# A four-layer transformer on one core: the byte distance between weights and activations in three feed-forwards

## The chip, the core and the metric

The kernel runs on one core of one Trainium2 chip. The metric is the device time of one execution in microseconds (us). A core has engines that run their own instruction streams and meet at semaphores: TensorE (PE) multiplies, VectorE (DVE) and ScalarE (ACT) work element by element, GpSimd (POOL) and SyncE (SP) here mostly issue transfers. All of them read the core's on-chip memory of 128 partitions; an address below is a byte address inside a partition.

## The reference

Input `x` is 512 tokens of width 1024, before which 16 learned tokens are put. Four layers follow, each a mixer and then a feed-forward: a recurrent unit with windowed attention, a retention, a gated delta rule, and a dilated attention. All is float32. Every feed-forward has hidden width 2816 and is

```python
def swiglu(h, w_in, w_out):
    gate, up = jnp.split(h @ w_in, 2, axis=-1)
    return (jax.nn.silu(gate) * up) @ w_out

h = (rms_norm(x, norm_ffn[layer]) * (1.0 + sc2) + sh2)
x = x + g2 * swiglu(h, w_ffn_in[layer], w_ffn_out[layer])
```

(the first two layers' feed-forwards have only a gain, and no shift and gate). The 16 learned tokens are dropped at the end; the last three feed-forwards work on the 512 tokens alone, the first one on all 528.

## The kernel before

Activations are kept transposed: the feature index, 128 at a time, is the partition, and the tokens run along the partition, so that a "chunk" of 128 features is 512 tokens, 2048 bytes. The residual stream `x_stream` stays on chip for the whole program.

A float32 product is made of three products of a rounded type (`F32R`): each operand is split in a high part and the rest, and `split_products` (lines 278 to 282) issues high times high (L280), high weights times low rows (L281) and low weights times high rows (L282) into the same accumulator:

```python
    nc.tensor.matmul(out, w_hi, h_hi, start=first, stop=False)
    nc.tensor.matmul(out, w_hi, h_lo, start=False, stop=False)
    return nc.tensor.matmul(out, w_lo, h_hi, start=False, stop=last)
```

In each, the 128 x 128 weights are the stationary operand, loaded by an instruction of its own (LDWEIGHTS, in the profile under PEld), and the rows, 512 tokens, are the moving operand that streams past them. In the profile's names the moving operand stands first: `ps<-up_h_hi,w_hi`.

Weights come from memory in tiles of up to 1 MB into `w_raw`, which has two slots. ACT copies a tile rounded into `w_hi` (`split_hi`, L195), DVE subtracts to get `w_lo` (`split_lo`, L201), and PE uses the tile as soon as `lo_ready` tells it. SP loads the tile after next when a slot is free. All of this is written out by hand: each engine has its own loop over the tiles, and semaphores (`tile_loaded`, `hi_ready`, `lo_ready`, `tile_used`, `psum_free`) join them.

A feed-forward (`feed_forward`, L892) has two parts. The first (`Up`, L777) normalizes the stream into `K.h_hi` and `K.h_lo` (8 chunks each), then goes over 22 tiles of weights; a tile gives one 128-wide chunk of gate and one of up, 2 outputs x 8 chunks x 3 = 48 matmuls. The first tile's 48 products are written by `Normalized.first_products` (lines 462, 463, 469), which has the first chunk in halves, and the other 21 tiles' by `split_products`, 1008 matmuls. ACT and DVE make `silu(gate) * up` and split it into `a_hi` and `a_lo` (22 chunks each). The second part (`add_projected`) multiplies these with the 16 half tiles of the down weights: 8 outputs x 22 chunks x 3 = 528 matmuls, and DVE adds each output to the stream.

Buffers are laid out by nesting: `K.sb` puts each new one right behind the one before it, and leaving a scope gives the space back. `take_h(name, ctx, cols, room)` puts an unused buffer of `room` bytes before `h_hi` and `h_lo`. Its sizes are the only things that shift the buffers of a feed-forward. `w_hi` starts at byte 49,792 and `w_lo` 16,384 bytes behind it, so both lie at 128 modulo 256; the 128 x 128 blocks inside them start 512 or 1024 bytes apart, and the chunks of 512 tokens 2048 bytes apart, all multiples of 256. So in a stage where rows are 512 tokens wide one number describes every matmul: D, the address of the weights minus the address of the moving rows, modulo 256.

| rows (512 wide) | address | D before |
|---|---|---|
| `ret_y`, `gdn_h`, `gdn_y`, `dsw_h` (mixers) | | 192 |
| `dsw_y` (output of the last mixer, 96 matmuls) | 126,272 | 64 |
| rows of feed-forwards 1, 2, 3 (`ffn1_h`, `up_2_h`, `up_3_h`) | 86,208 | 192 |
| activations of feed-forwards 1, 2, 3 (`up_1_act`, `up_2_act`, `up_3_act`) | 118,976 | 192 |

Three stages are different. In feed-forward 0 a chunk is 528 tokens, 2112 bytes, used as two spans of 264 tokens: D goes down by 64 from chunk to chunk and by 32 from the first span to the second, so the first span has D = 192, 128, 64, 0 in turn and the second 160, 96, 32, 224. In the values of the retention (`w_hi,ret_h_hi`) and of the first group of the last mixer (`w_hi,dsw_h_hi`) the roles are exchanged: 256 columns of weights move, and 128 tokens of the rows are stationary. Weights and rows are there 0 and 192 apart.

Of the kernel before, what the change touches and what calls it, by code (L numbers as in the profile page):

```python
# [28 lines left out]
P = 128  # L29
# [29 lines left out]
ONLY_X = (N_META, 1)  # L59
# [6 lines left out]
class Chain:  # L66


    def __init__(self, sem):
        self.sem, self.n = sem, 0  # L70
# [706 lines left out]
class Up:  # L777

    def __init__(self, K, up, cols, norm, side, ctx, cond=False):
        self.K, self.up, self.cols, self.side, self.cond = K, up, cols, side, cond
        W = T - cols[0]
        self.n = {k: v[1] for k, v in K.up.items()}
        self.sems = {k: v[0] for k, v in K.up.items()}
        self.a_hi = K.sb(up.name + "_act_hi", [P, FF_CH, W], F32R, ctx)
        self.a_lo = K.sb(up.name + "_act_lo", [P, FF_CH, W], F32R, ctx)
        self.work = K.sb(up.name + "_work", [P, 3 * W], ctx=ctx)
        self.silu, self.prod = self.work[:, 0:W], self.work[:, W:3 * W].rearrange("p (n w) -> p n w", n=2)
        if side is not None:  # L790
            side.open(ctx)
        gain, shift = norm
        self.norm = Normalized(K, cols, gain, shift, side and side.acc[:].rearrange("p n c -> p (n c)"), ctx)
        for k in K.up:
            K.up[k][1] += up.tiles
# [93 lines left out]
            pe.wait_ge(self.sems["lo"], self.n["lo"] + self.up.tiles)  # L889


def feed_forward(K, up, down, cols, gate=None, side=None, norm=None, stats=True, cond=False, two_ahead=False):  # L892


    with ExitStack() as ctx:
        first = Up(K, up, cols, norm, side, ctx, cond)
        add_projected(K, down, (first.a_hi, first.a_lo), cols, parts=2, base=cols[0], gate=gate, side=side,
                      before=first, stats=Squares(K, cols, first.work, down) if stats else None, two_ahead=two_ahead)


def column_weights(name, matrix, tiles, unroll, cols=256, first=0, split=True):

    rows = matrix.shape[0] // P
    rowwise = matrix.rearrange("(k p) c -> p k c", p=P)

    def source(i, j):
        at = first + j * cols + i * (unroll * cols)
        return [(lambda slot: slot.rearrange("p (k c) -> p k c", k=rows), rowwise[:, :, bass.ds(at, cols)])]
    w = Weights(name, tiles, unroll, (rows, cols), source, split)
    w.loads = 1  # L910
    return w


def up_weights(name, matrix):

    rowwise = matrix.rearrange("(k p) c -> p k c", p=P)

    def source(i, j):
        def part(g):
            return lambda slot: slot.rearrange("p (k g c) -> p k g c", k=DC, g=2)[:, :, g, :]  # L920
        return [(part(g), rowwise[:, :, bass.ds(i * (2 * P) + (j * P + g * D_FF), P)]) for g in range(2)]
    w = Weights(name, FF_CH, 2, (DC, 2 * P), source)
    w.loads = 2
    return w


def down_weights(name, matrix):

    rows = FF_CH // 2
    halves = matrix.rearrange("(h k p) c -> h p k c", p=P, h=2)  # L930

    def source(i, j):
        return [(lambda slot: slot.rearrange("p (k c) -> p k c", k=rows),
                 halves[j % 2][:, :, bass.ds(i * (2 * P) + (j // 2) * P, P)])]
    w = Weights(name, 2 * DC, 4, (rows, P), source)
    w.loads = 1
    return w
# [252 lines left out]
def param(K, name, n):  # L1190
    at = K.at[name]
    return K.cols[:, at:at + n]
# [1951 lines left out]
def delta_rule(K, I, W, mods):  # L3144
    gain, shift, gate = mods
    with ExitStack() as layer:
        rule = DeltaRule(K, I, W, gain, shift, layer)
        stats = Squares(K, ONLY_X, rule.squares, W["gdn_out"])
        add_projected(K, W["gdn_out"], (rule.y_hi, rule.y_lo), ONLY_X, base=N_META, gate=gate, before=rule, stats=stats)
# [637 lines left out]
def two_blocks(nc, I, const, out):  # L3787
    with ExitStack() as ctx:
        K = Core(nc, ctx)
        K.const = const  # L3790
        ab = I["ab_w_in"].rearrange("a d n -> (a d) n")
        ret = I["ret_w_in"].rearrange("a d n -> (a d) n")
        W = {}
        W["ab_x"] = column_weights("ab_x", ab, 2, 2)
        W["ab_q"] = column_weights("ab_q", ab, 2, 2, first=1024)
        W["ab_k"] = column_weights("ab_k", ab, 1, 1, P, first=1536)
        W["ab_v"] = column_weights("ab_v", ab, 1, 1, P, first=1664)
        W["ab_g"] = column_weights("ab_g", ab, 2, 2, first=512)
        W["ab_out"] = column_weights("ab_out", I["ab_w_out"][0], 4, 2)
        W["up_0"], W["down_0"] = up_weights("up_0", I["ffn_w_gu"][0]), down_weights("down_0", I["ffn_w_down"][0])  # L3800
        W["ret_k"] = column_weights("ret_k", ret, 4, 2, first=D)
        W["ret_q"] = column_weights("ret_q", ret, 4, 2)
        W["ret_v"] = column_weights("ret_v", ret, 8, 2, first=2 * D)
        W["ret_g"] = column_weights("ret_g", ret, 8, 2, first=4 * D)
        W["ret_out"] = column_weights("ret_out", I["ret_w_out"][0], 8, 2, P)
        W["up_1"], W["down_1"] = up_weights("up_1", I["ffn_w_gu"][1]), down_weights("down_1", I["ffn_w_down"][1])
        gdn = I["gdn_w_in_2"].rearrange("a d n -> (a d) n")
        W["gdn_k0"] = column_weights("gdn_k0", gdn, 1, 1, first=D)
        W["gdn_ab"] = gate_weights("gdn_ab", gdn)
        W["gdn_k"] = column_weights("gdn_k", gdn, 3, 3, first=D + 256)  # L3810
        W["gdn_q"] = column_weights("gdn_q", gdn, 4, 2)
        W["gdn_v"] = column_weights("gdn_v", gdn, 4, 2, first=2 * D)
        W["gdn_z"] = column_weights("gdn_z", gdn, 4, 2, first=3 * D)
        W["gdn_out"] = column_weights("gdn_out", I["gdn_w_out_2"][0], 4, 2)
        W["up_2"], W["down_2"] = up_weights("up_2", I["w_ffn_in_2"][0]), down_weights("down_2", I["w_ffn_out_2"][0])
        dsw = I["dsw_w_in_2"].rearrange("a d n -> (a d) n")
        W["dsw_qk"] = column_weights("dsw_qk", dsw, 12, 2)
        for g in range(3):
            W["dsw_v%d" % g] = column_weights("dsw_v%d" % g, dsw, 2, 2, first=3072 + g * 512)
        W["dsw_out"] = column_weights("dsw_out", I["dsw_w_out_2"][0], 2, 2, 512)  # L3820
        W["up_3"], W["down_3"] = up_weights("up_3", I["w_ffn_in_2"][1]), down_weights("down_3", I["w_ffn_out_2"][1])
        K.plan(list(W.values()))

        prologue(K, I, list(W.values())[0])
        with ExitStack() as layer:
            K.take_h("ab_h", layer)
            gate = K.sb("ab_gate", [P, LRU_CH, T], ctx=layer)
            norm = Normalized(K, ALL, param(K, "norm_ab", 8), space=gate[:].rearrange("p c w -> p (c w)"))
            mixer = Mixer(K, I, W, norm, gate, layer)
            add_projected(K, W["ab_out"], (K.h_hi, K.h_lo), ALL, before=mixer, stats=Squares(K, ALL, mixer.work, W["ab_out"]))  # L3830
        K.end_layer()
        with ExitStack() as layer:
            K.take_h("ffn0_h", layer)
            feed_forward(K, W["up_0"], W["down_0"], ALL, norm=(param(K, "norm_ffn", 16)[:, 0:8], None), cond=True)
        retention(K, W)
        K.end_layer()
        mods = [Modulation(K, I, 0, ctx)]
        with ExitStack() as layer:
            K.take_h("ffn1_h", layer, ONLY_X, 960)
            feed_forward(K, W["up_1"], W["down_1"], ONLY_X, side=mods[0],  # L3840
                         norm=(param(K, "norm_ffn", 16)[:, 8:16], None), two_ahead=True)
        delta_rule(K, I, W, mods[0].parts(0))
        K.end_layer()
        mods.append(Modulation(K, I, 1, ctx))
        modulated_feed_forward(K, W["up_2"], W["down_2"], mods[0].parts(1), mods[1])
        dilated_attention(K, I, W, mods[1].parts(0))
        K.end_layer()
        modulated_feed_forward(K, W["up_3"], W["down_3"], mods[1].parts(1), stats=False)
        store(K, out)


def modulated_feed_forward(K, up, down, mods, side=None, stats=True):
    gain, shift, gate = mods
    with ExitStack() as layer:
        K.take_h(up.name + "_h", layer, ONLY_X, 896)
        feed_forward(K, up, down, ONLY_X, gate, side, (gain, shift), stats)


def store(K, out):
# [50 lines left out]
```

## Time and profile before

| | |
|---|---|
| median of three runs | 3008.45 us (3006.57 to 3008.66) |
| profiled execution, first to last instruction | 3006.2 us |
| PE busy | 2891.8 us (96%) |
| PE weight load busy | 2484.8 us (83%) |
| DVE busy | 1437.2 us (48%) |
| ACT busy | 1121.2 us (37%) |
| POOL busy | 118.6 us (4%) |
| mean granted clock of PE | 0.985 |

The span is one execution. "Busy" of an engine is the time in which at least one of its instructions was under way. A matmul's duration in this profile is from its start to a modelled end, and matmuls overlap: what PE gets done is read from the distance between the starts of two matmuls, not from a duration. Stages are given in us from the start of the span: feed-forward 1 has its 1008 products from 1132.2 to 1370.0 and its 528 from 1370.1 to 1496.7; feed-forward 2 from 1916.3 to 2154.0 and 2154.2 to 2280.3; feed-forward 3 from 2644.1 to 2874.7 and 2875.0 to 2995.6.

### The profile page before, as it was taken

To read this page: it belongs to the slowest core of one execution; us is meant where nothing else is said; L and a number is where in the kernel's file an instruction comes from. 1 tells how busy PE (TensorE), PEld (TensorE's weight loads), DVE (VectorE), ACT (ScalarE), POOL (GpSimd) and SP (SyncE) were. 2 spreads that over 40 slices of the span, in tenths; PEclk is the share of its full clock that TensorE was granted. 3 is DMA by queue.
4 is the path that set the end of the run, shared out by engine and by line. 5 is a ranking of instruction groups with operands and counts; after the bars stand their busy time and mean duration, and the time that the engine had idled before them with its cause. 6 is when DMAs were issued, how large, how long until landed. Compare 5 with 4: busy or idle time off the path is not lost. (4 is left out here: it accounts for less than half of the span.)

```text
span 3006.2 us, 39600 instructions
## 1 busy us (share of the span) xinstructions
PE 2891.8 (96%) x16454; PEld 2484.8 (83%) x16454; DVE 1437.2 (48%) x1613; ACT 1121.2 (37%) x1551; POOL 118.6 (4%) x116
## 2 busy tenths in 40 slices
PE   8989999999999899999999988999999999899999
PEld 8889999998987587888877787788887887778887
DVE  5664333233513734444477745545455865643322
ACT  5444332132232324331265434343224446543321
POOL 0000000001300000000000010000001310000000
PEclk9999999999999999999999999999999999999999
DMA  4212332322222135556432220455563431033322
GB/s 132 66 43 71 92 90 77 97 95 92 70 84 71 28 95 147 156 154 175 132 105 85 70 43 29 112 161 155 166 181 101 112 99 32 18 95 98 94 87 86
DMA packets 409379, 292.70 MB, mean 97 GB/s; under 512 B 24851, under 2 KB 388180, under 8 KB 409250
## 3 DMA queue, kind: packets, MB, share of 16 engines
q1 hardware_dynamic: 403210, 286.68, 32.8%
q0 software_dynamic: 1600, 3.55, 0.8%
q8 instruction: 95, 1.56, 0.2%
q10 hardware_dynamic: 4440, 0.64, 0.2%
q14 instruction: 34, 0.28, 0.0%
HBM read 286.16 MB, written 4.13 MB: 97 GB/s over the span
## 5 line engine op out<-in xcount | busy, mean ns | idle before, releaser
L201 DVE TENSOR_TENSOR w_lo<-w_raw,w_hi 128x2048 fp32r<-128x2048 f32 (+2 forms) x237 | 498.9, 2105 | 523.5 <-ACT w_hi L195 523.0
L195 ACT ACTIVATE w_hi<-w_raw 128x2048 fp32r<-128x2048 f32 (+2 forms) x237 | 416.4, 1757 | 261.8 <-PE ps L282 152.0
L280 PE MATMUL ps<-ffn_h_hi,w_hi 128*128 128x264 f32 (+1 forms) x1008 | 324.9, 322 | 5.2 <-DVE w_lo L201 5.2
L282 PE MATMUL ps<-ffn_h_hi,w_lo 128*128 128x264 f32 (+1 forms) x1008 | 324.0, 321 | 0.0
L281 PE MATMUL ps<-ffn_h_lo,w_hi 128*128 128x264 f32 (+1 forms) x1008 | 322.8, 320 | 0.0
L282 PE MATMUL ps<-up_act_hi,w_lo 128*128 128x512 f32 (+1 forms) x880 | 307.5, 349 | 0.0
L280 PE MATMUL ps<-up_act_hi,w_hi 128*128 128x512 f32 (+1 forms) x880 | 307.1, 349 | 0.2 <-DVE w_lo L201 0.2
L281 PE MATMUL ps<-up_act_lo,w_hi 128*128 128x512 f32 (+1 forms) x880 | 306.4, 348 | 0.0
L280 PE MATMUL ps<-up_h_hi,w_hi 128*128 128x512 f32 x672 | 263.1, 392 | 4.8 <-DVE w_lo L201 4.8
L282 PE MATMUL ps<-up_h_hi,w_lo 128*128 128x512 f32 x672 | 265.1, 394 | 0.0
L281 PE MATMUL ps<-up_h_lo,w_hi 128*128 128x512 f32 x672 | 263.3, 392 | 0.0
L833 DVE TENSOR_TENSOR up_work<-up_work,ps 128x512 f32<-128x512 f32 (+1 forms) x88 | 60.9, 692 | 422.4 <-ACT up_work L814 422.4
L814 ACT ACTIVATE up_work<-ps 128x512 f32<-128x512 f32 (+1 forms) x88 | 53.0, 602 | 527.2 <-PE ps L282 527.1
L280 PEld LDWEIGHTS ps<-ffn_h_hi,w_hi 128*128 128x128 f32 x1008 | 190.5, 189 | 19.0 <-DVE w_lo L201 5.8
L281 PEld LDWEIGHTS ps<-ffn_h_lo,w_hi 128*128 128x128 f32 x1008 | 190.9, 189 | 14.3
L282 PEld LDWEIGHTS ps<-ffn_h_hi,w_lo 128*128 128x128 f32 x1008 | 190.8, 189 | 14.1
L281 PEld LDWEIGHTS ps<-up_act_lo,w_hi 128*128 128x128 f32 x880 | 165.4, 188 | 22.3
L280 PEld LDWEIGHTS ps<-up_act_hi,w_hi 128*128 128x128 f32 x880 | 165.4, 188 | 21.7 <-DVE w_lo L201 0.6
L282 PEld LDWEIGHTS ps<-up_act_hi,w_lo 128*128 128x128 f32 x880 | 165.6, 188 | 21.2
L280 PEld LDWEIGHTS ps<-up_h_hi,w_hi 128*128 128x128 f32 x672 | 126.6, 188 | 32.9 <-DVE w_lo L201 5.7
L281 PEld LDWEIGHTS ps<-up_h_lo,w_hi 128*128 128x128 f32 x672 | 126.5, 188 | 29.0
L282 PEld LDWEIGHTS ps<-up_h_hi,w_lo 128*128 128x128 f32 x672 | 126.6, 188 | 26.6
(580 smaller groups left out, 5620.4 us busy)
## 6 DMA issues: line engine op xcount, KB each, us to landing
mod_raw<-in_w_ada_dram SPq DMA_DIRECT2D x128, 384.0 KB, 4.0
w_raw<-in_ffn_w_gu_dram SPq DMA_DIRECT2D x88, 512.0 KB, 5.2
w_raw<-in_w_ffn_in_dram SPq DMA_DIRECT2D x88, 512.0 KB, 5.2
w_raw<-in_ret_w_in_dram SPq DMA_DIRECT2D x24, 1024.0 KB, 5.2
w_raw<-in_ffn_w_down_dram SPq DMA_DIRECT2D x32, 704.0 KB, 4.9
w_raw<-in_w_ffn_out_dram SPq DMA_DIRECT2D x32, 704.0 KB, 4.9
w_raw<-in_dsw_w_in_dram SPq DMA_DIRECT2D x18, 1024.0 KB, 5.1
w_raw<-in_gdn_w_in_dram SPq DMA_DIRECT2D x16, 1024.0 KB, 5.7
```

What stands on the lines that cost most here:

```text
L195: self.nc.scalar.activation(self.w_hi[:, s, 0:w.size], self.raw[:, s, 0:w.size], ACT.Copy).then_inc(self.hi_ready, 1)
L201: self.nc.vector.tensor_tensor(self.w_lo[:, s, 0:w.size], self.raw[:, s, 0:w.size], self.w_hi[:, s, 0:w.size].bitcast(F32), ALU.subtract). ...
L280: nc.tensor.matmul(out, w_hi, h_hi, start=first, stop=False)
L281: nc.tensor.matmul(out, w_hi, h_lo, start=False, stop=False)
L282: return nc.tensor.matmul(out, w_lo, h_hi, start=False, stop=last)
L814: nc.scalar.activation(K.spans(self.silu, self.cols), K.out_psum((j % 2) * 2, self.cols), ACT.Silu).then_inc(sems["silu"], 1)
L833: nc.vector.tensor_tensor(K.spans(self.prod[:, j % 2, :], self.cols), K.spans(self.silu, self.cols), K.out_psum((j % 2) * 2 + 1, self.cols ...
```

## The change

No instruction is added, removed or reordered; only buffers move. `room` before the rows gets new sizes (960 to 896 bytes; 896 to 768; 896 to 800), and a second unused buffer, `act_room`, of 128, 160 and 64 bytes comes between the rows and the activations.

| matmuls | buffer | address before | after | D before | D after |
|---|---|---|---|---|---|
| 1056 | `ffn1_h_hi`, `_lo` | 86,208 | 86,144 | 192 | 0 |
| 528 | `up_1_act_hi`, `_lo` | 118,976 | 119,040 | 192 | 128 |
| 1056 | `up_2_h_hi`, `_lo` | 86,208 | 86,080 | 192 | 64 |
| 528 | `up_2_act_hi`, `_lo` | 118,976 | 119,008 | 192 | 160 |
| 1056 | `up_3_h_hi`, `_lo` | 86,208 | 86,112 | 192 | 32 |
| 528 | `up_3_act_hi`, `_lo` | 118,976 | 118,944 | 192 | 224 |

(Addresses are those of `_hi`; `_lo` starts a multiple of 256 bytes behind.) What stands behind the activations in the same scope moves with them by 64, 32 or 32 bytes: `up_n_work`, the buffers of the modulation (`mod_raw`, `mod_acc`) in feed-forwards 1 and 2, and `normed_8` in feed-forward 3.

```diff
-    def __init__(self, K, up, cols, norm, side, ctx, cond=False):
+    def __init__(self, K, up, cols, norm, side, ctx, cond=False, act_room=0):
...
+        if act_room:
+            K.sb(up.name + "_act_room", [P, act_room // 4], ctx=ctx)
         self.a_hi = K.sb(up.name + "_act_hi", [P, FF_CH, W], F32R, ctx)
...
-            K.take_h("ffn1_h", layer, ONLY_X, 960)
+            K.take_h("ffn1_h", layer, ONLY_X, 896)
             feed_forward(K, W["up_1"], W["down_1"], ONLY_X, side=mods[0],
-                         norm=(param(K, "norm_ffn", 16)[:, 8:16], None), two_ahead=True)
+                         norm=(param(K, "norm_ffn", 16)[:, 8:16], None), two_ahead=True, act_room=128)
...
-        modulated_feed_forward(K, W["up_2"], W["down_2"], mods[0].parts(1), mods[1])
+        modulated_feed_forward(K, W["up_2"], W["down_2"], mods[0].parts(1), mods[1], h_room=768, act_room=160)
...
-        modulated_feed_forward(K, W["up_3"], W["down_3"], mods[1].parts(1), stats=False)
+        modulated_feed_forward(K, W["up_3"], W["down_3"], mods[1].parts(1), stats=False, h_room=800, act_room=64)
...
-def modulated_feed_forward(K, up, down, mods, side=None, stats=True):
+def modulated_feed_forward(K, up, down, mods, side=None, stats=True, h_room=0, act_room=0):
     gain, shift, gate = mods
     with ExitStack() as layer:
-        K.take_h(up.name + "_h", layer, ONLY_X, 896)
-        feed_forward(K, up, down, ONLY_X, gate, side, (gain, shift), stats)
+        K.take_h(up.name + "_h", layer, ONLY_X, h_room)
+        feed_forward(K, up, down, ONLY_X, gate, side, (gain, shift), stats, act_room=act_room)
```

## Rows read from the trace of the kernel before

**Rows 1.** The page: span, and busy time of the engines.

```profile
span 3006.2 us, 39600 instructions
PE 2891.8 (96%) x16454; PEld 2484.8 (83%) x16454; DVE 1437.2 (48%) x1613; ACT 1121.2 (37%) x1551; POOL 118.6 (4%) x116
```

**Rows 2.** Groups by form, PE: line, names, shapes, count | busy, mean ns | idle before.

```profile
L280 PE MATMUL ps<-up_h_hi,w_hi 128*128 128x512 f32 x672 | 263.1, 392 | 4.8 <-DVE w_lo L201 4.8
...
L280 PE MATMUL ps<-up_act_hi,w_hi 128*128 128x512 f32 x528 | 207.0, 392 | 0.2 <-DVE w_lo L201 0.2
...
L280 PE MATMUL ps<-ffn_h_hi,w_hi 128*128 128x512 f32 x336 | 132.8, 395 | 2.8 <-DVE w_lo L201 2.8
```

**Rows 3.** Windows, PE: stretch, length, busy (count), clock, DMA share, GB/s.

```profile
1132.20:1370.00 237.80, 237.73 (x1056) 0.99 0.55 156
1370.10:1496.70 126.60, 126.40 (x576) 1.00 0.56 160
1916.30:2154.00 237.70, 237.63 (x1055) 0.99 0.55 156
2154.20:2280.30 126.10, 126.10 (x577) 1.00 0.57 166
2644.10:2874.70 230.60, 230.53 (x1007) 1.00 0.35 96
2875.00:2995.60 120.60, 120.60 (x528) 1.00 0.27 78
```

**Rows 4.** Timeline, PE and PEld, feed-forward 2, D 192: start, duration, instruction.

```profile
2099.81 0.39 PE L282 MATMUL ps<-up_h_hi,w_lo 128*128 128x512 f32 x1
2099.81 0.19 PEld L280 LDWEIGHTS ps<-up_h_hi,w_hi 128*128 128x128 f32 x1
...
2102.79 0.39 PE L280 MATMUL ps<-up_h_hi,w_hi 128*128 128x512 f32 x1
...
2108.28 0.39 PE L280 MATMUL ps<-up_h_hi,w_hi 128*128 128x512 f32 x1
```

**Rows 5.** Timeline, PE, output product of the last mixer, D 64, 24 matmuls apart.

```profile
2603.87 0.40 PE L280 MATMUL ps<-dsw_y_hi,w_hi 128*128 128x512 f32 x1
...
2609.47 0.40 PE L280 MATMUL ps<-dsw_y_hi,w_hi 128*128 128x512 f32 x1
```

**Rows 6.** Timeline, PE, values, roles exchanged: distance 0, then 192; 15 matmuls apart.

```profile
797.95 0.28 PE L280 MATMUL ps<-w_hi,ret_h_hi 128*128 128x256 f32 x1
...
799.75 0.28 PE L280 MATMUL ps<-w_hi,ret_h_hi 128*128 128x256 f32 x1
...
2439.95 0.28 PE L280 MATMUL ps<-w_hi,dsw_h_hi 128*128 128x256 f32 x1
...
2441.65 0.28 PE L280 MATMUL ps<-w_hi,dsw_h_hi 128*128 128x256 f32 x1
```

**Rows 7.** Timeline, PE, feed-forward 0: starts of five outputs in turn, 24 matmuls apart.

```profile
375.99 0.28 PE L280 MATMUL ps<-ffn_h_hi,w_hi 128*128 128x264 f32 x1
...
378.88 0.29 PE L280 MATMUL ps<-ffn_h_hi,w_hi 128*128 128x264 f32 x1
...
381.81 0.28 PE L280 MATMUL ps<-ffn_h_hi,w_hi 128*128 128x264 f32 x1
...
384.70 0.29 PE L280 MATMUL ps<-ffn_h_hi,w_hi 128*128 128x264 f32 x1
...
387.64 0.28 PE L280 MATMUL ps<-ffn_h_hi,w_hi 128*128 128x264 f32 x1
```

**Rows 8.** The page, groups: the splits of the weight tiles on DVE and ACT.

```profile
L201 DVE TENSOR_TENSOR w_lo<-w_raw,w_hi 128x2048 fp32r<-128x2048 f32 (+2 forms) x237 | 498.9, 2105 | 523.5 <-ACT w_hi L195 523.0
L195 ACT ACTIVATE w_hi<-w_raw 128x2048 fp32r<-128x2048 f32 (+2 forms) x237 | 416.4, 1757 | 261.8 <-PE ps L282 152.0
```

**Rows 9.** Timeline, PE, third mixer's projections, D 192, 20 matmuls apart.

```profile
1577.04 0.40 PE L281 MATMUL ps<-gdn_h_lo,w_hi 128*128 128x512 f32 x1
...
1581.71 0.40 PE L280 MATMUL ps<-gdn_h_hi,w_hi 128*128 128x512 f32 x1
```

More of the change, by code:

```diff
@@ L889, in row_ready, with feed_forward @@
             pe.wait_ge(self.sems["lo"], self.n["lo"] + self.up.tiles)
-def feed_forward(K, up, down, cols, gate=None, side=None, norm=None, stats=True, cond=False, two_ahead=False):
+def feed_forward(K, up, down, cols, gate=None, side=None, norm=None, stats=True, cond=False, two_ahead=False,
+                 act_room=0):
     with ExitStack() as ctx:
-        first = Up(K, up, cols, norm, side, ctx, cond)
+        first = Up(K, up, cols, norm, side, ctx, cond, act_room)
         add_projected(K, down, (first.a_hi, first.a_lo), cols, parts=2, base=cols[0], gate=gate, side=side,
```

## The prediction

> **What bounds the kernel now.** I read the page's busy times first, then the groups by form, then windows over the stages that the change touches, then the timeline inside them. PE is busy for 2891.8 of 3006.2 us, DVE for 48%, ACT for 37% [rows 1]. The reader is to see that these stages have hardly any idle time to give back or to hide in: over the whole program PE stood idle for 4.8, 2.8 and 0.2 us in total before the first products of the rows and activations [rows 2]. The six stages of the change take 237.8, 126.6, 237.7, 126.1, 230.6 and 120.6 us, together 1079.4 us, at a granted clock of 0.99 to 1.00, that is at the 2.4 GHz level throughout [rows 3]. So the time of a stage is the number of its matmuls times the distance between two starts. In the cleanest stage, the rows of feed-forward 3, 1007 matmuls lie in 230.60 us, 229.0 ns apiece, and in a steady piece 24 matmuls take 2108.28 - 2102.79 = 5.49 us, 228.8 ns [rows 3, 4]. At 2.4 GHz, 512 columns by themselves are 213.3 ns. Some 15.5 ns per matmul are something else. The load of the next weights starts within 10 ns of the matmul that it runs beside, and reads the same memory at the same time [rows 4]. Whether these two reads disturb each other, and how that depends on D, is the whole question, because the change does nothing else.
>
> **The change, part by part.** It adds and removes no instruction on any engine or queue. It changes D for 1056 + 528 matmuls in each of three feed-forwards, 4752 in all (1008 by the shared helper and 48 of the first tile, then 528). I price each new D against D = 192 with the nearest rows.
>
> *D = 64, rows of feed-forward 2, 1056 matmuls.* The trace has this very case: the last mixer's output product, 512 columns, D = 64. There 24 matmuls take 2609.47 - 2603.87 = 5.60 us, 233.3 ns [rows 5]. Against 228.9 (the middle of the two figures above) that is 4.4 ns more: 1056 x 4.4 = 4.6 us.
>
> *D = 0, rows of feed-forward 1, 1056 matmuls.* The nearest row has the roles exchanged, 256 columns of weights moving over 128 stationary tokens. At distance 0, 15 matmuls take 799.75 - 797.95 = 1.80 us, 120.0 ns; at distance 192 they take 2441.65 - 2439.95 = 1.70 us, 113.3 ns [rows 6]. That is 6.7 ns for distance 0, an upper end; the lower end is nothing, as the roles differ. I take half, 3.3 ns: 3.5 us.
>
> *D = 128, activations of feed-forward 1, 528 matmuls.* No row has it alone. Between nothing and the 4.4 ns of D = 64 I take 2.2 ns: 1.2 us.
>
> *D = 32, 160, 224: rows of feed-forward 3, activations of 2 and 3, 2112 matmuls.* These are odd multiples of 32. Feed-forward 0 has them side by side with the even ones: its four outputs per tile are the same 24 matmuls of 264 columns, the first and third over D = 192, 128, 64, 0, the second and fourth over 160, 96, 32, 224. They take 2.89, 2.93, 2.89 and 2.94 us [rows 7]. This is 2.0 ns per matmul for an odd multiple over the mean of the even ones. The mean of the even ones is itself above D = 192, by (0 + 4.4 + 3.3 + 2.2) / 4 = 2.5 ns on my prices. So the term lies between 2.0 and 4.5 ns, or higher if 512 columns pay more often than 264. I take 3.3 ns: 2112 x 3.3 = 7.0 us.
>
> *Everything else costs nothing.* The splits of the weight tiles read and write buffers that don't move; one tile of 48 matmuls is 48 x 229 = 11.0 us of PE, against 2105 ns of DVE and 1757 ns of ACT for the split [rows 8]. The elementwise work on moved buffers has the rest of 11 us as cover. If that cover were gone, PE would wait on `w_lo` at L201, which it does for 4.8 us in total now [rows 2]. The modulation's transfer buffers move by 64 and 32 bytes; DMA is busy for 0.55 of feed-forwards 1 and 2 [rows 3], and a tile is asked for two tiles ahead, so a small slowdown there is hidden as well. A slower PE makes this cover larger. Nothing waits on PE that could turn its delay into more than itself: it adds one to one.
>
> Sum: 4.6 + 3.5 + 1.2 + 7.0 = 16.3 us. The profiled execution has a span of 3006.2 us, 2.3 us under the median of 3008.45; the terms are differences, so I add them to the median: 3024.8 us.
>
> A rule of the Trainium skill speaks against all of this. The page "TensorE: Matmul & The Clock Gate", section "Step-by-step: what each phase is for", says that the engine has two independent read ports into on-chip memory and that loading the next weights "doesn't steal SBUF read bandwidth from the running matmul". By it D would be without effect, and the sum would be 0. The trace disagrees in part: equal matmuls differ with their addresses in rows 7 (2.89 against 2.93 and 2.94 us) and rows 6.
>
> **The rivals.**
>
> *A: D does not decide, the time stays.* The mechanism is that a stream of matmuls falls into one of several steady rhythms after each interruption, and the rhythm, not the address, sets the distance. For it: at D = 192, in the third mixer, 20 matmuls take 1581.71 - 1577.04 = 4.67 us, 233.5 ns, the same as at D = 64 [rows 9]. So the one row from which I priced D = 64 may be a rhythm too. Against it: at D = 192 this rhythm is rare, since the cleanest stage of 1007 matmuls averages 229.0 ns [rows 3], while feed-forward 0 repeats its 2.89 and 2.93 us output after output [rows 7]. It gives 3008.5 us, within 0.2% (6 us) of now; 0.2% is also about what a measurement of this kernel can tell from no change. The independent ports of the skill's page lead to the same time. Chance 0.17, with the cases in which gains and losses of the six stages cancel.
>
> *B: faster.* Some distances may be better than 192. The smallest excess over pure streaming in my rows is 113.3 - 106.7 = 6.6 ns (256 columns at 2.4 GHz are 106.7 ns) [rows 6], against 15.6 ns at 512 columns and D = 192. If the four distances without a row of their own at any width (32, 128, 160, 224; 2640 matmuls) reached it, they would give 2640 x 9.0 = 23.8 us back, while D = 64 and D = 0 still cost 8.1 us: 2992.8 us. It decides once the mean over the 4752 matmuls is below 229 ns, and counts as faster from 1.3 ns below. Against it: rows 7 puts the odd distances above the even ones. Chance 0.07.
>
> *C: a larger loss.* With 512 columns the moving read meets the load at more points than with 264, and every distance but 64 may pay the full 6.7 ns of rows 6: 3696 x 6.7 + 4.6 = 29.4 us, 3037.9 us; at 9 ns for the odd ones it would be 3042.7 us. For it: at 264 columns the four even distances are mixed and each lasts three matmuls only, so that rows 7 may hide much of a steady effect. Against it: no 512-column row of the trace has more than 233.5 ns. Chance 0.12.
>
> *D: the change does not do what it says.* The address arithmetic gives the six distances exactly, and no rule moves the buffers back. I give this nothing.
>
> **How the numbers follow.** The forecast (a loss between 6 and 27 us, likeliest 16.3) has 0.64, C 0.12, A 0.17, B 0.07. Slower by over 0.2% is 0.64 + 0.12 = 0.76, within it 0.17, faster 0.07. The range must leave out 2 in 10 at most. Its low end is 3009: D = 64 as in rows 5 and nothing else would be 3013.1, and I reach into A down to its centre. Its high end is 3037, just under C as worked out. That leaves out B, the lower half of A and most of C's upper part.
>
> **What would show it.** In the windows of rows 3, taken again after the change, the stages should grow by 1056 x 3.3 = 3.5 us (rows of feed-forward 1), 1.2 (its activations), 4.6 and 1.7 (feed-forward 2), 3.5 and 1.7 (feed-forward 3). The timeline should show 233.3 ns per matmul in the rows of feed-forward 2, steadily, and between 229 and 236 elsewhere; the stages of the mixers and of feed-forward 0, which keep their addresses, should not move. PE's idle time before L280 should stay under 5 us per group, and the clock at 0.99 to 1.00. I am wrong in the mechanism if the rows of feed-forward 2 keep 229 ns, wrong in the sizes if one of the stages gains or if one pays over 6.7 ns per matmul, and wrong about the cover if DVE or ACT becomes what PE waits for.

## The result, and the profile after

The changed kernel takes 3019.44 us (median of 4 runs, 3015.91 to 3021.02), against 3007.84 us for the kernel before in the same comparison (median of 4, 3006.57 to 3008.66). The ratio is 1.004, with a 95% interval of 1.0027 to 1.0052: 11.6 us slower, where 16.3 us were forecast. The two lines of the page that answer to [rows 1], of the changed kernel:

```profile
span 3018.6 us, 39600 instructions
PE 2903.2 (96%) x16454; PEld 2483.4 (82%) x16454; DVE 1437.1 (48%) x1613; ACT 1120.6 (37%) x1551; POOL 118.7 (4%) x116
```

Same instructions on every engine, 11.4 us more of busy PE, nothing on DVE and ACT. The six stages of the change, as windows of the changed kernel (stretch, length, PE busy with count, clock, DMA share, GB/s), which answer to [rows 3]:

```profile
1132.90:1368.40 235.50, 235.50 (x1055) 0.99 0.55 158
1368.70:1496.50 127.80, 127.80 (x576) 1.00 0.55 158
1913.50:2155.50 242.00, 241.99 (x1056) 0.99 0.54 153
2155.70:2284.00 128.30, 128.30 (x577) 1.00 0.56 163
2648.20:2884.80 236.60, 236.60 (x1008) 0.99 0.34 94
2885.00:3008.00 123.00, 123.00 (x529) 1.00 0.26 77
```

Line by line against [rows 3] that is -2.3, +1.2, +4.3, +2.2, +6.0 and +2.4 us, together +13.8 us. The first line is the surprise: the rows of feed-forward 1, now at D = 0, got faster. Of the fifth line's 6.0 us only some 4.5 come from D. The clock of that window is 0.99 where it was 1.00 before. PE has just waited 3.0 us for `w_lo`, and soon after that seven matmuls start 427 ns apart, at the 1.2 GHz level:

```profile
2648.77 0.63 PE L282 MATMUL ps<-up_h_hi,w_lo 128*128 128x512 f32 x1
2649.20 0.63 PE L280 MATMUL ps<-up_h_hi,w_hi 128*128 128x512 f32 x1
```

Before, such a stretch fell into the first tile, ahead of the window, where it only made the wait that follows shorter; inside the window it costs about 1.6 us.

The span grew by 12.4 us, so some 1.4 us came back elsewhere. The largest piece is the core of the third mixer, between its projections and its output product, where this change moves nothing. That stretch took 118.2 us before, at a granted clock of 0.93, and 115.4 us after, at 0.95. In the kernels below that do not edit this mixer it took 113.4 us (clock 0.96, lo_apart) to 119.2 us (0.92, halves). So its length goes mostly with the time that PE spends at the 1.2 GHz level in it, though not exactly (both_shifted has 115.9 us at 0.93). A smaller piece goes the other way: the first of the two weight tiles in the values of the last mixer, which keeps its addresses, went from 113.6 to 117.8 ns per matmul, 0.4 us more.

The timeline of the changed kernel shows the two new rhythms (start, duration, instruction). First the rows of feed-forward 1, D = 0, 21 matmuls apart; then the rows of feed-forward 3, D = 32, 24 matmuls apart:

```profile
1304.03 0.39 PE L280 MATMUL ps<-ffn_h_hi,w_hi 128*128 128x512 f32 x1
...
1308.79 0.39 PE L280 MATMUL ps<-ffn_h_hi,w_hi 128*128 128x512 f32 x1
...
2749.68 0.40 PE L282 MATMUL ps<-up_h_hi,w_lo 128*128 128x512 f32 x1
...
2755.28 0.40 PE L282 MATMUL ps<-up_h_hi,w_lo 128*128 128x512 f32 x1
```

4.76 us / 21 = 226.7 ns, and 5.60 us / 24 = 233.3 ns. Taking the mean distance of two starts over a whole stage, gaps of 260 ns and more left out, the changed kernel has 226.9 (D = 0), 232.5 (128), 233.3 (64), 233.3 (160), 233.3 (32) and 233.3 ns (224), where the kernel before had 228.9 to 229.0 in all six. The excess over 512 columns at 2.4 GHz (213.3 ns) was 15.6 ns and is 13.6 ns at D = 0, 19.2 ns at 128 and 20.0 ns at the other four.

### The profile page after: what moved, and what is told of

The parts are those of the page before. It is cut to its first block and busy times, and to the rows that moved or that the text cites. A ratio compares the mean times of both kernels' runs of the same rounds, so it can differ in the third digit from the quotient of the medians.

```text
span 3018.6 us, 39600 instructions
## 1 busy us (share of the span) xinstructions
PE 2903.2 (96%) x16454; PEld 2483.4 (82%) x16454; DVE 1437.1 (48%) x1613; ACT 1120.6 (37%) x1551; POOL 118.7 (4%) x116
## 5 line engine op out<-in xcount | busy, mean ns | idle before, releaser
L280 PE MATMUL ps<-ffn_h_hi,w_hi 128*128 128x264 f32 (+1 forms) x1008 | 323.9, 321 | 5.2 <-DVE w_lo L201 5.2
L282 PE MATMUL ps<-ffn_h_hi,w_lo 128*128 128x264 f32 (+1 forms) x1008 | 322.9, 320 | 0.0
L280 PE MATMUL ps<-up_act_hi,w_hi 128*128 128x512 f32 (+1 forms) x880 | 309.9, 352 | 0.0
L282 PE MATMUL ps<-up_act_hi,w_lo 128*128 128x512 f32 (+1 forms) x880 | 308.2, 350 | 0.0
L280 PE MATMUL ps<-up_h_hi,w_hi 128*128 128x512 f32 x672 | 267.6, 398 | 6.1 <-DVE w_lo L201 6.1
L282 PE MATMUL ps<-up_h_hi,w_lo 128*128 128x512 f32 x672 | 267.1, 398 | 0.0
L280 PEld LDWEIGHTS ps<-ffn_h_hi,w_hi 128*128 128x128 f32 x1008 | 190.5, 189 | 19.0 <-DVE w_lo L201 5.9
L282 PEld LDWEIGHTS ps<-ffn_h_hi,w_lo 128*128 128x128 f32 x1008 | 190.8, 189 | 13.3
L282 PEld LDWEIGHTS ps<-up_act_hi,w_lo 128*128 128x128 f32 x880 | 165.6, 188 | 24.4
L280 PEld LDWEIGHTS ps<-up_act_hi,w_hi 128*128 128x128 f32 x880 | 165.4, 188 | 23.4 <-DVE w_lo L201 0.2
L280 PEld LDWEIGHTS ps<-up_h_hi,w_hi 128*128 128x128 f32 x672 | 127.1, 189 | 37.4 <-DVE w_lo L201 7.0
L282 PEld LDWEIGHTS ps<-up_h_hi,w_lo 128*128 128x128 f32 x672 | 126.9, 189 | 30.8
```

## The experiments

Where a kernel starts from the kernel before or from the changed one, the diff is against that. Means "per matmul" are distances between starts as above, worked out from every start in the trace of the one profiled execution of a kernel. Lines left out of a code cut are marked "...". "Before" in each comparison is 3006 to 3008 us.

### All feed-forwards at distance 0

```diff
-                         norm=(param(K, "norm_ffn", 16)[:, 8:16], None), two_ahead=True, act_room=128)
+                         norm=(param(K, "norm_ffn", 16)[:, 8:16], None), two_ahead=True, act_room=0)
...
-        modulated_feed_forward(K, W["up_2"], W["down_2"], mods[0].parts(1), mods[1], h_room=768, act_room=160)
+        modulated_feed_forward(K, W["up_2"], W["down_2"], mods[0].parts(1), mods[1], h_room=832, act_room=0)
...
-        modulated_feed_forward(K, W["up_3"], W["down_3"], mods[1].parts(1), stats=False, h_room=800, act_room=64)
+        modulated_feed_forward(K, W["up_3"], W["down_3"], mods[1].parts(1), stats=False, h_room=832, act_room=0)
```

> Rows and activations of all three feed-forwards at D = 0. Theory T1 (D alone sets the distance between two matmul starts; D = 0 gives 226.8 ns, as the rows of feed-forward 1 showed after the change): all six stages at 226.8 ns, 4752 x (229.0 - 226.8) = 10.5 us less than the kernel before, about 2997.4 us, and some 22 us less than the changed kernel. Rival T2 (the rhythm is a matter of the stage, of what stands around it, not of D): only the rows of feed-forward 1 at 226.8 ns, the activations still at 232 to 233 ns and the rows of 2 and 3 at 229 to 233 ns, 3007 to 3019 us.

2998.71 us (median of 6) against 3007.59, ratio 0.9967 (0.9955 to 0.9979): 8.9 us faster than before, and faster than the changed kernel. Windows of this run, the same six stages:

```profile
1132.20:1367.80 235.60, 235.58 (x1056) 0.99 0.55 158
1368.00:1493.70 125.70, 125.37 (x577) 1.00 0.56 161
1912.90:2148.50 235.60, 235.55 (x1055) 0.99 0.56 158
2148.80:2274.40 125.60, 125.28 (x576) 1.00 0.56 167
2639.10:2867.50 228.40, 228.39 (x1007) 1.00 0.35 97
2867.80:2987.20 119.40, 119.40 (x528) 1.00 0.27 79
```

Each is shorter than before, by 2.2, 0.9, 2.1, 0.5, 2.2 and 1.2 us: 9.1 us together. All six have 226.7 to 227.1 ns per matmul. T1 holds, T2 falls; the total is 8.9 us less where T1 had 10.5. The first two feed-forwards' activations gain less than the 1.2 us of the third, as they share PE with the sums of the modulation, and waits take part of it.

### The distances dealt out anew

```diff
-            K.take_h("ffn1_h", layer, ONLY_X, 896)
+            K.take_h("ffn1_h", layer, ONLY_X, 768)
...
-                         norm=(param(K, "norm_ffn", 16)[:, 8:16], None), two_ahead=True, act_room=128)
+                         norm=(param(K, "norm_ffn", 16)[:, 8:16], None), two_ahead=True, act_room=32)
...
-        modulated_feed_forward(K, W["up_2"], W["down_2"], mods[0].parts(1), mods[1], h_room=768, act_room=160)
+        modulated_feed_forward(K, W["up_2"], W["down_2"], mods[0].parts(1), mods[1], h_room=832, act_room=64)
...
-        modulated_feed_forward(K, W["up_3"], W["down_3"], mods[1].parts(1), stats=False, h_room=800, act_room=64)
+        modulated_feed_forward(K, W["up_3"], W["down_3"], mods[1].parts(1), stats=False, h_room=736, act_room=32)
```

> The distances dealt out anew: feed-forward 1 rows 128, activations 96; feed-forward 2 rows 0, activations 192; feed-forward 3 rows 96, activations 64. T1: 232.5 ns for the rows of feed-forward 1, 226.8 for the rows of 2, 229.0 for the activations of 2, 233.3 for the activations of 3; D = 96 was in no 512-wide stage so far, by its neighbours 64 and 128 some 233 ns. T2: each stage keeps what it had after the change, 226.8, 232.5, 233.3, 233.3, 233.3, 233.3.

One run, 3021.4 us. Windows:

```profile
1132.40:1371.90 239.50, 239.47 (x1055) 1.00 0.55 155
1372.10:1500.90 128.80, 128.80 (x576) 1.00 0.55 157
1920.40:2155.80 235.40, 235.40 (x1056) 0.99 0.56 158
2156.00:2282.60 126.60, 126.36 (x576) 1.00 0.56 165
2649.80:2885.80 236.00, 236.00 (x1007) 1.00 0.34 94
2886.10:3009.00 122.90, 122.90 (x528) 1.00 0.27 77
```

Per matmul: 232.4 (128), 234.2 (96), 226.7 (0), 229.0 (192), 234.3 (96), 233.3 ns (64). Every distance took its rhythm along to its new stage; feed-forward 2's rows went from 242.0 to 235.4 us and its activations from 128.3 to 126.6. D = 96 is the worst multiple of 32. In these six stages D decides, and the stage does not.

### Weights and rows moved together

```diff
+        self.sb("w_shift", [P, 16])
         self.raw = self.sb("w_raw", [P, 2, SLOT])
```

> The kernel before with 64 unused bytes ahead of the weight buffers, so that weights and rows both move by 64 bytes and every D stays. T1: every stage as before, 229.0 ns in the three feed-forwards and 233.3 ns in the last mixer's output product; about 3008 us. Rival T3 (the absolute address of the rows decides, not the distance): the rows move as they did from D 192 to 128, so the feed-forwards go to 232.5 ns, 4752 x 3.5 = 16.6 us more.

One run, 3007.0 us. Windows of the last output product (D = 64) and of feed-forward 3 (D = 192):

```profile
2595.90:2618.50 22.60, 22.55 (x99) 1.00 0.17 46
2642.90:2873.50 230.60, 230.60 (x1007) 1.00 0.35 96
2873.70:2994.40 120.70, 120.70 (x529) 1.00 0.27 78
```

The two stages of feed-forward 3 are as in [rows 3] to 0.1 us, at 228.9 ns, with every address 64 bytes further, and feed-forward 2 and the activations of feed-forward 1 have 228.9 to 229.0 ns as well. T3 falls, since it had 232.5 ns for all of them: the distance counts, and this shift of the absolute addresses changed nothing.

One stage is not as before, which T1 alone does not explain. The rows of feed-forward 1 (D = 192, as ever) took 0.9 us more than in [rows 3] (first the window, then starts from its timeline; line 281 is L280 of the kernel before):

```profile
1133.20:1371.90 238.70, 238.70 (x1056) 0.99 0.56 156
...
1150.21 0.40 PE L281 MATMUL ps<-ffn_h_hi,w_hi 128*128 128x512 f32 x1
...
1155.81 0.40 PE L281 MATMUL ps<-ffn_h_hi,w_hi 128*128 128x512 f32 x1
...
1200.39 0.39 PE L281 MATMUL ps<-ffn_h_hi,w_hi 128*128 128x512 f32 x1
...
1205.88 0.39 PE L281 MATMUL ps<-ffn_h_hi,w_hi 128*128 128x512 f32 x1
```

The pairs are 24 matmuls apart: 5.60 us, 233.3 ns each, in the first five weight tiles (240 matmuls), and 5.49 us, 228.8 ns each, in the rest. The change comes at 1190.8 us, where twelve small matmuls of the modulation interrupt the stream. So one stage with one D can run in either of two rhythms; the one at D = 192 that [rows 9] shows for some 50 matmuls can last much longer.

### Fewer stationary columns

```diff
...
-                        hi[:, k, m * P:(m + 1) * P], lo[:, k, m * P:(m + 1) * P],
+                        hi[:, k, m * P:m * P + held], lo[:, k, m * P:m * P + held],
```

with `held` 64 in the up products and 32 in the down products, and the output on as many partitions; otherwise the changed kernel.

> The changed kernel with fewer stationary columns in its last three feed-forwards: 64 of 128 in the up products and 32 of 128 in the down products (the other output features are not computed, so the output is not the reference's). The load of the weights is then a half and a quarter as long; the moving operand stays 512 columns. T1a (the excess over 213.3 ns is made of collisions of the moving read with the load of the next weights, 6.7 ns each, two or three of them in a load of 128 columns): about half the excess with 64 columns, 218 to 224 ns, and 213 to 220 ns with 32. Rival T4 (the excess belongs to the matmul and its addresses, whatever the load's length): the intervals of the changed kernel, 226.8, 232.5, 233.3, 233.3, 233.3, 233.3.

One run, 3015.1 us. Windows of the rows of feed-forward 1 and the activations of feed-forward 3, and one of the loads in the latter:

```profile
1132.50:1369.40 236.90, 236.90 (x1056) 1.00 0.55 157
2879.80:3002.80 123.00, 123.00 (x529) 1.00 0.27 77
...
L280 PEld LDWEIGHTS ps<-up_act_hi,w_hi 128*32 128x32 f32 x174 | 18.8, 108 | 21.8
```

A load's record falls from 188 ns (128 columns) to 134 (64) and 108 ns (32), and not to a half and a quarter as the expectation had it.

Per matmul: 230.0 (D = 0, 64 columns), 230.7 (128, 32), 232.0 (64, 64), 233.2 (160, 32), 231.7 (32, 64), 233.3 ns (224, 32). T1a fails: with half or a quarter of the weights to load the excess is not half or a quarter but 16.7 to 20.0 ns, and at D = 0 it even rose from 13.6 to 16.7 ns. T4 comes nearer (two stages are the same to 0.1 ns), though four moved by 1.3 to 3.1 ns, so the load seems to have some part in the rhythm. A caution comes from a stage that this run leaves alone, the output product of the third mixer (D = 192). Its matmuls, once at 2.4 GHz, are 233.3 ns apart to the end of the stage (24 matmuls in 5.60 us), where the other kernels with D = 192 there have 228.9 to 229.0 ns:

```profile
1859.65 0.40 PE L280 MATMUL ps<-gdn_y_hi,w_hi 128*128 128x512 f32 x1
...
1865.25 0.40 PE L280 MATMUL ps<-gdn_y_hi,w_hi 128*128 128x512 f32 x1
```

A shift of a few ns in a single stage of a single run can thus be a change of rhythm and nothing else.

### Half as many moving columns

```diff
...
+                        for a in (0, 256):
+                            mm = split_products(
+                                nc, K.ps[:, (j % 2) * 2 + m, a:a + 256],
+                                hi[:, k, m * P:(m + 1) * P], lo[:, k, m * P:(m + 1) * P],
+                                K.h_hi[:, k, a:a + 256], K.h_lo[:, k, a:a + 256], k == 0 and a == 0, k == DC - 1 and a == 256)
```

and the same in the down products, from all_zero.

> As all_zero, but the 512 moving columns of the products in the last three feed-forwards (after their first weight tile) go in two matmuls of 256 columns, at D = 0. It does the same arithmetic with twice the matmuls. If the excess is one sum per matmul (226.7 - 213.3 = 13.4 ns): 106.7 + 13.4 = 120.1 ns per matmul, so 240 ns for what took 226.7, and 4608 x 13.4 = 62 us more. If it goes with the columns: 113.3 ns per matmul, and the total stays at 2999 us.

One run, 3059.4 us, 60.7 us over all_zero where 62 were expected. Windows of feed-forward 3:

```profile
2677.00:2920.40 243.40, 243.37 (x2015) 0.99 0.33 91
2920.50:3047.10 126.60, 126.60 (x1057) 1.00 0.26 75
```

The down products start 120 ns apart, every one of them, and so do the up products once the clock is at 2.4 GHz (their window begins with a stretch at 1.2 GHz). That is 106.7 + 13.3 ns: the excess is paid once per matmul, and is the same for 256 and 512 columns at D = 0.

### Low weights 64 bytes apart from high ones

```diff
+        self.sb("w_lo_shift", [P, 16])
         self.w_lo = self.sb("w_lo", [P, 2, SLOT], F32R)
```

from all_zero, with 64 bytes less room before the rows.

> As all_zero, but the low halves of the weights 64 bytes behind the high ones modulo 256, so that in the feed-forwards the high weights are at 0 and the low weights at 64 from the rows. Theory T5 (the moving read of one matmul meets the load of the next one's weights): of the three products, L280 and L282 run beside a load of high weights and keep 226.7 ns to the next start, L281 runs beside the load of low weights and gets about 233.3 ns. Rival T6 (a matmul's own weights and rows decide): L282, the one with low weights, is the long one. In both cases the mean is near 228.9 ns, and the total near 3008 us, unless a disturbed product throws its neighbours out of rhythm as well; that would show as a mean above 230 ns.

One run, 3025.6 us, where both theories had some 3008. Its total also holds the mixers, whose rows moved with everything behind the weights and went from 228.9 to 233.2 ns. In the timeline of the down products of feed-forward 3 (lines 281 to 283 are L280 to L282 of the kernel before):

```profile
2949.96 0.39 PE L282 MATMUL ps<-up_act_lo,w_hi 128*128 128x512 f32 x1
2950.19 0.40 PE L283 MATMUL ps<-up_act_hi,w_lo 128*128 128x512 f32 x1
2950.43 0.39 PE L281 MATMUL ps<-up_act_hi,w_hi 128*128 128x512 f32 x1
```

The product with low weights is followed after 0.24 us, the others after 0.23. Over the stage: 228.3, 229.1 and 235.9 ns, mean 231.1. The long one is the product whose own weights are at 64, as T6 said and T5 did not; but the two at D = 0 lost 1.6 and 2.4 ns against the 226.7 ns of all_zero as well, and the mean is 231.1 ns where both theories had 228.9. The expectation had named a mean above 230 ns as the sign that a disturbed product throws its neighbours out of rhythm too.

### The same, and the low rows apart too

```diff
+        if room > 256 and name != "dsw_h":
+            self.sb(name + "_lo_shift", [P, 16], ctx=ctx)
         self.h_lo = self.sb(name + "_lo", [P, DC, pitch or T - cols[0]], F32R, ctx)
...
+        if act_room:
+            K.sb(up.name + "_act_lo_shift", [P, 16], ctx=ctx)
         self.a_lo = K.sb(up.name + "_act_lo", [P, FF_CH, W], F32R, ctx)
```

The rooms before rows and activations are changed so that the high rows keep D = 0.

> As lo_apart (low weights 64 bytes behind the high ones), and the low rows and low activations of the last three feed-forwards moved by the same 64 bytes. Now L281 (high weights, low rows; line 281 or 282 of this kernel) has its own weights and rows at D = 192, L282 (low weights, high rows) at 64, L280 at 0. But each matmul's moving rows and the weights loaded beside it, which are the next matmul's, are again all at distance 0: high rows with high weights, low rows with low weights, high rows with high weights. T5 (the moving read meets the load of the next weights): 226.8 ns for all three, as in all_zero. T6 (a matmul's own weights and rows decide): the product with low weights stays long, near 235 ns, and the one with low rows goes to 229 or more; a mean of 230 ns or above, as in lo_apart (230.9 to 231.2) or worse.

One run, 3028.7 us. The same place in its timeline (lines 283 to 285):

```profile
2949.93 0.39 PE L285 MATMUL ps<-up_act_hi,w_lo 128*128 128x512 f32 x1
2950.16 0.40 PE L283 MATMUL ps<-up_act_hi,w_hi 128*128 128x512 f32 x1
2950.39 0.39 PE L284 MATMUL ps<-up_act_lo,w_hi 128*128 128x512 f32 x1
```

Over the stage 232.6 (own distance 0), 231.7 (192) and 229.1 ns (64), mean 231.1. T5 falls for good: pairing each moving read with the next load at distance 0 does not bring 226.8 back. T6 said 230 ns or above for the mean, which came, but has the order wrong: now the product with low weights is the short one. Its mean is not a sum of single prices either: own distances of 0, 192 and 64 would give (226.8 + 229.0 + 233.3) / 3 = 229.7 ns. So neither simple pairing explains the single intervals. What the runs do give is a mean for a stage in which all three distances are equal.

### Distances that are no multiple of 32

```diff
+        whole = self.sb(name, [P, chunks * cols + 64], F32R, ctx)
+        return whole[:, nudge // 4:nudge // 4 + chunks * cols].rearrange("p (c w) -> p c w", c=chunks)
```

> Distances that are no multiple of 32, by starting the rows inside a longer buffer: feed-forward 1 rows 16, activations 240; feed-forward 2 rows 48, activations 208; feed-forward 3 rows 4, activations 8. Theory T7 (what counts is whether the rows start on the same 64-byte piece grid as the weights: 0, 64, 128, 192 are special): 4, 8, 16, 48, 208 and 240 all cost as much as 32 or 224, 233.3 ns. Rival T8 (the cost changes smoothly with the distance, so that near 0 it is near that of 0): 4 and 8 stay at 227 ns, 16 and 240 lie between 227 and 233, 48 between those of 32 and 64.

One run, 3024.6 us. Windows of the rows of feed-forward 1 and of the two stages of feed-forward 3:

```profile
1133.60:1376.60 243.00, 242.98 (x1056) 1.00 0.54 153
2656.00:2889.90 233.90, 233.86 (x1008) 0.99 0.34 95
2890.10:3012.10 122.00, 122.00 (x529) 1.00 0.27 77
```

Per matmul: 235.8 (16), 231.6 (240), 234.6 (48), 232.1 (208), 230.6 (4), 231.5 ns (8). T7 falls: 4 and 8 cost less than 32. T8 is right about the order near 0 for 4, 8 and 240 but not about the size: one float off costs 3.8 ns already, and 16 is worse than 32, as 48 is worse than 32 and 64. The 235.8 ns of D = 16 are a mean of two rhythms, as in both_shifted: the first 240 matmuls are 233.3 ns apart, and those behind the first sums of the modulation 236.7 ns.

All distances seen with 512 moving rows, with the mean of a stage. Those for 4, 8, 16, 32, 48, 160, 208, 224 and 240 come from one stage in one kernel each (leaving out narrow), and after both_shifted and narrow a difference of a few ns between two of these is not sure to be one of D. 0, 64, 96, 128 and 192 came in two stages or more:

| D | 0 | 4 | 8 | 16 | 32 | 48 | 64 | 96 | 128 | 160 | 192 | 208 | 224 | 240 |
|---|---|---|---|---|---|---|---|---|---|---|---|---|---|---|
| ns | 226.8 | 230.6 | 231.5 | 235.8 | 233.3 | 234.6 | 233.3 | 234.3 | 232.5 | 233.3 | 229.0 | 232.1 | 233.3 | 231.6 |

### The mixers at distance 0 as well

```diff
-            K.take_h("ret_h", inputs, ALL, 192, 576)
+            K.take_h("ret_h", inputs, ALL, 128, 576)
...
-        K.sb("gdn_line_rest", [P, 8], ctx=ctx)
+        K.sb("gdn_line_rest", [P, 56], ctx=ctx)
...
+        K.sb("dsw_y_room", [P, 16], ctx=layer)
         y = [K.sb("dsw_y_" + n, [P, ATT_CH, SEQ], F32R, layer) for n in ("hi", "lo")]
```

The feed-forwards are as in all_zero.

> All feed-forwards at D = 0 as in the run all_zero (2998.7 us), and in addition the third mixer's rows and gated values and the last mixer's output rows at D = 0 (from 192, 192, 64) and the retention's rows at D = 0 in its 512-wide stages (from 192), which puts its values, with exchanged roles, at 64 instead of 0. If the distance is all that counts: 984 x 2.2 = 2.2 us from the third mixer, 576 x 2.2 = 1.3 us from the retention, 96 x 6.6 = 0.6 us from the last output product, and from the values of the retention (120.0 ns now, 768 matmuls of 128 stationary columns) between nothing and 5.1 us, as the only other distance seen there, 192, has 113.3 ns. 2989.5 to 2994.6 us. If another distance inside the mixers (their small matmuls, whose addresses move with them) costs as much as this gives, 2998.7 us or more.

2988.0 us (median of 6) against 3006.96, ratio 0.9933 (0.9917 to 0.9949): it beats both kernels, and all_zero, and lies 1.5 us under the range that was expected. Windows of the retention's values, its gate and the third mixer's projections:

```profile
734.50:845.00 110.50, 110.50 (x960) 1.00 0.25 81
847.50:934.50 87.00, 86.99 (x384) 1.00 0.31 97
1502.30:1716.80 214.50, 209.55 (x941) 1.00 0.28 79
```

and the same stages of the kernel before:

```profile
735.00:851.30 116.30, 116.28 (x960) 0.99 0.24 77
853.90:941.70 87.80, 87.79 (x384) 1.00 0.31 96
1514.50:1729.80 215.30, 211.00 (x940) 1.00 0.28 79
```

The largest piece is the values, where the roles are exchanged: 116.3 to 110.5 us, of which 1.6 is the clock (0.99 against 1.00; permuted, with the same addresses there and clock 1.00, has 114.7 us) and 4.2 the move of that distance from 0 to 64, most intervals falling from 120 to 113 ns. The gate and the projections give 0.8 us each, and the last output product 0.3 (22.5 to 22.2 us). Of the 10 us between the two ratios these windows and the retention's queries (0.4 us) account for 6.5. Much of the rest of the profiled execution is the core of the third mixer: 113.9 us here, at a clock of 0.96, against 118.0 in all_zero. Its moved addresses aren't needed for that: lo_apart, which does not edit this mixer, has 113.4 us at the same clock, and the next run, with the addresses of this one, has 115.1 us at 0.94.

### The last mixer's rows too

```diff
-                K.take_h("dsw_h", proj, ONLY_X, 896)
+                K.take_h("dsw_h", proj, ONLY_X, 832)
```

on top of the kernel of the run before.

> As the run mixers (2988.0 us), with the last mixer's rows at D = 0 instead of 192 as well. Its 720 matmuls of 512 columns should go from 229.1 to 226.8 ns, 1.7 us less; its 192 with exchanged roles go from distance 192 (113.5 ns) to 0, at which the retention's values had 120.0 ns, 1.2 us more. Together 0.4 us less, which no comparison of total times here can tell from nothing; the stages' own lengths should show both.

2990.86 us (median of 5) against 3006.15, ratio 0.9944 (0.9930 to 0.9957), not to be told from the run before it. Windows of the last mixer's 512-wide projections and of its values:

```profile
2281.80:2411.70 129.90, 129.90 (x572) 1.00 0.44 115
2411.90:2435.70 23.80, 23.80 (x196) 1.00 0.17 55
```

In the run before they were 131.2 and 22.6 us: 1.3 us gained by the products with moving rows and 1.2 us lost by those with exchanged roles, both as expected. So the best distance depends on the product: 0 is best for 512 moving rows, and the worst of the three seen (0, 64, 192) for 256 moving columns of weights.

## Why the prediction was right, and where it was not

**What bounds the kernel** held. PE's time per matmul is all there is to change, it adds one to one, and the clock stayed at 0.99 to 1.00 in the six stages. Of what keeps its addresses, the core of the third mixer moved by 2.8 us all the same, with its clock. The cover held too: DVE and ACT are as busy as before, and PE's waits on `w_lo` before L280 over the whole program (engine and line, what it waited for, us in total, times, longest) are, for the kernel before and for the changed one:

```profile
PE ps L280 <- DVE w_lo L201: 11.6, 7, 3.2
```

```profile
PE ps L280 <- DVE w_lo L201: 13.0, 7, 3.0
```

That is 1.4 us more, small beside the 13.8 us of the windows, and no new wait: it is the one before the second tile of feed-forward 3, whose first tile no longer runs at 1.2 GHz. The group of [rows 2] that had 4.8 us has 6.1 us for that reason, over the 5 us that I had set as a limit. The prediction also took those 4.8 us for all of PE's waiting on `w_lo`; they were that one group's, and the whole was 11.6 us.

**D = 64**: 4.4 ns and 4.6 us were forecast; 233.3 ns and 4.3 us came. This term was read from a row with the same distance, width and roles [rows 5], and it was right to 0.3 us. Both_shifted and narrow show that the doubt about a single short row was fair: at D = 192 such a row can have 233.3 ns too.

**D = 0**: the term that failed, in its sign. I took half of the 6.7 ns by which distance 0 exceeds 192 in [rows 6], 3.5 us of loss; it was a gain of 2.1 ns and 2.3 us. The row itself was sound: halves shows the same 120.0 ns with 256 moving columns of rows. The error was to carry over a difference. The distance 192, to which I compared, has an excess of 6.6 ns at 256 columns in exchanged roles and of 15.6 ns at 512; the distance 0 has 13.3 ns in both. Had I added the excess of that row to 213.3 ns, I would have had 226.7 ns, which is what came. That is hindsight, and no rule: the excess of the row at 192 carried over in the same way gives 219.9 ns, where 228.9 were in the trace.

**D = 128**: 2.2 ns forecast, 3.5 ns measured. The window grew by 1.2 us, as forecast, but only by luck: 528 x 3.5 ns is 1.8 us, and the gaps left out of the mean were 0.7 us shorter.

**D = 32, 160, 224**: 3.3 ns forecast, 4.3 to 4.4 ns measured, near the upper end of 4.5 that I had named. Feed-forward 0 mixes distances, and [rows 7] showed the order but not the full size.

By the measured ns per matmul the stages with a loss were priced 2.8 us too low (12.8 for 15.6) and D = 0 was 5.7 us too high (3.5 for -2.2). The sum would be 13.4 us, within the measured 11.6 (8.1 to 15.6 by the interval); the forecast of 16.3 was above it. That the total came within 5 us is in part luck, as the two errors have opposite signs. By the signs that the prediction set for itself the sizes were wrong, as one of the stages gained; the mechanism stood, as the rows of feed-forward 2 went to 233.3 ns.

Rival A (rhythm, not address) falls as an account of the change, with all_zero and permuted: the mean of a stage follows D from stage to stage. What it says of rhythms is true beside that. At D = 192 the 233.3 ns of [rows 9] came for 240 matmuls in both_shifted and for nearly a whole stage in narrow. What picks one rhythm or the other is not known; in both_shifted and sixteens the change came at an interruption of the stream. Rival B named the right mechanism for the wrong distances: a distance better than 192 exists, and it is 0. C falls: none of the six distances cost more than 4.4 ns over 192; those that do (96, 48 and 16, with 5.3, 5.6 and 6.8 ns) are not among them. The rule of the Trainium skill, page "TensorE: Matmul & The Clock Gate", section "Step-by-step: what each phase is for", that the weight load doesn't take read bandwidth from the running matmul, would have made the change free. The runs contradict the conclusion, as moving only the rows costs up to 9 ns; whether it is bandwidth of the load that is lost they leave open, since a load of a quarter of the columns did not help (narrow) and pairing with the next load did not either (pairs_apart).

## What to carry to other kernels

When PE is the bound and its matmuls start further apart than their columns explain, compare the addresses of the two operands modulo 256: unused buffers of a few dozen to a few hundred bytes moved this kernel by 0.4% one way, and by 0.3% (the feed-forwards) and 0.7% (the mixers too, in part chance of the clock) the other. Measure the distances for the shape at hand, as 0 is best for 512 moving rows and the worst of three for 256 moving columns of weights. Do not carry a price over from another shape: here neither the difference between two distances nor the excess over pure streaming held for every D. And read a spacing from more than one stage, as the same D can show two rhythms.

## What the runs showed of the hardware

- The mean distance between the starts of two 128 x 512 matmuls at 2.4 GHz was 226.7 to 235.8 ns in a stage of a feed-forward, against 213.3 ns of columns. For D = 0, 64, 96 and 128 it repeated to 0.4 ns in different feed-forwards and kernels; for D = 192 it was 228.9 to 229.1 ns nearly always, but 229.9 ns in one stage of both_shifted.
- At one D the stream can stand in more than one rhythm: 228.9 or 233.3 ns at D = 192 (both_shifted, and the third mixer's output in narrow), 233.3 or 236.7 ns at D = 16 (sixteens).
- 64 and 320 bytes modulo 512 (rows of feed-forward 2 after the change; output of the last mixer) both have 233.3 ns, while 64 and 192 differ: that is what supports a period of 256, and no more was tried.
- Moving both operands by 64 bytes left the stages of feed-forward 3 at 230.6 and 120.7 us; no other common shift was tried.
- At D = 0 the excess is 13.4 to 13.8 ns per matmul at 512 and 13.3 ns at 256 columns, so splitting a matmul in two costs one more of it (60.7 us for 4608 more matmuls).
- A load of 64 or 32 stationary columns in place of 128 does not remove the excess, and went with a slower D = 0 in the one stage that had it (226.9 to 230.0 ns with 64).
- One float of displacement (D = 4) costs 3.8 ns. Which two reads meet, and when, was not found.
